# Eight modulation units moved from the front of a two-block transformer kernel into its projection and attention steps

## The reference, cut to what matters

```python
def first_block(x, c, ..., ada_w, ada_b, w_in, ...):
    c_act = jax.nn.silu(c)
    mod = c_act @ ada_w[l] + ada_b[l]
    sh1, sc1, g1, sh2, sc2, g2 = jnp.split(mod, 6, axis=-1)
    h = rmsnorm(x, norm1_g[l]) * (1.0 + sc1[:, None]) + sh1[:, None]
    x = x + g1[:, None] * token_mixer(h, w_in[l], ...)
    h = rmsnorm(x, norm2_g[l]) * (1.0 + sc2[:, None]) + sh2[:, None]
    x = x + g2[:, None] * moe_ffn(h, ...)
    return rmsnorm(x, final_g)
```

## Time and profile before

| | |
|---|---|
| runs | 3006.77, 3005.53, 2999.02 us; median 3005.53 us |
| profiled execution | 2999.47 us, span 2997.7 us |
| busy | PE 2752.5 us (92%), DVE 1880.2 us (63%), ACT 1278.0 us (43%) |
| clock of TensorE granted | 0.956 of full speed over the span |
| read from HBM | 635.59 MB, 214 GB/s over the span |

### The profile page before, as it was taken

How to read it: one execution, slowest core, us unless ns; L and a number is a source line. 1 busy time by engine, 2 the same in 40 slices (tenths; PEclk the granted TensorE clock), 3 DMA queues, 4 the chain that set the end, 5 groups by cost and what they waited for, 6 DMA issues and landing times.

```text
span 2997.7 us, 36656 instructions
## 1 busy us (share of the span) xinstructions
PE 2752.5 (92%) x14444; PEld 2296.5 (77%) x14444; DVE 1880.2 (63%) x2345; ACT 1278.0 (43%) x1540; POOL 24.4 (1%) x46
## 2 busy tenths in 40 slices
PE   3769999897999999999699898999899999999997
PEld 0258898676788787877499396999778888888886
DVE  6986665566666788898766444444555455445444
ACT  2024543342444577777433053534344444443443
POOL 0000000000000000000000000000000000000000
PEclk9789998797999999999899997999999999999999
DMA  8787674340777899999444252544355655555553
GB/s 326 297 319 262 245 272 165 109 173 33 254 258 248 292 324 370 368 369 370 162 168 169 83 190 89 183 177 182 140 196 168 193 187 194 187 195 190 189 197 112
DMA packets 178526, 644.87 MB, mean 215 GB/s; under 512 B 10923, under 2 KB 10988, under 8 KB 134104
## 3 DMA queue, kind: packets, MB, share of 16 engines
q1 hardware_dynamic: 170208, 593.53, 55.7%
q0 software_dynamic: 5344, 30.93, 2.8%
q10 hardware_dynamic: 2840, 18.56, 1.7%
HBM read 635.59 MB, written 7.39 MB: 214 GB/s over the span
## 4 chain that ended last, share of the span: by engine, by line
PE 73%; DVE 12%; DMA 8%; ACT 3%; issue 2%; DVEq 0%; ACTq 0%; SPq 0%
PE ps L1570 72%; DMA raw<-in_stream 7%; DVE w_lo L914 3%; DVE raw L993 2%; ACT w_hi L579 2%; DVE arena L975 0%; DVE arena L973 0%; DVE arena L1073 0%; DVE arena L1089 0%; DVE arena L1475 0%; DVE h_lo L965 0%; PE ps L1704 0%; DVE arena L1473 0%; DVE arena L1474 0%; PE ps L2061 0%
## 5 line engine op out<-in xcount | busy, mean ns | idle before, releaser
L914 DVE TENSOR_TENSOR w_lo<-raw,w_hi 128x1024 fp32r<-128x1024 f32 x968 | 1171.4, 1224 | 803.6 <-ACT w_hi L579 801.0
L579 ACT ACTIVATE w_hi<-raw 128x1024 fp32r<-128x1024 f32 x968 | 1011.8, 1057 | 946.3 <-PE ps L1570 853.2
L1570 PE MATMUL ps<-w_hi,h_hi 128*128 128x512 f32 x1216 | 477.0, 392 | 16.2 <-DVE h_lo L1529 10.0
L1570 PE MATMUL ps<-w_hi,r_hi 128*128 128x512 f32 x1184 | 469.2, 396 | 13.9 <-DVE w_lo L914 5.7
L1570 PE MATMUL ps<-w_lo,h_hi 128*128 128x512 f32 x1216 | 475.0, 391 | 0.0
L1570 PE MATMUL ps<-w_hi,h_lo 128*128 128x512 f32 x1216 | 475.0, 391 | 0.0
L1570 PE MATMUL ps<-w_hi,r_lo 128*128 128x512 f32 x1184 | 462.8, 391 | 0.0
L1570 PE MATMUL ps<-w_lo,r_hi 128*128 128x512 f32 x1184 | 462.8, 391 | 0.0
L1570 PE MATMUL ps<-h_hi,w_hi 128*128 128x256 f32 x1536 | 441.6, 287 | 11.5 <-DVE h_lo L965 3.9
L1570 PE MATMUL ps<-h_lo,w_hi 128*128 128x256 f32 x1536 | 438.1, 285 | 0.0
L1570 PE MATMUL ps<-h_hi,w_lo 128*128 128x256 f32 x1536 | 437.9, 285 | 0.0
(11 more groups left out here) (270 smaller groups left out, 1898.1 us busy)
## 6 DMA issues: line engine op xcount, KB each, us to landing
raw<-in_stream SPq DMA_DIRECT2D x524, 1024.0 KB, 5.5
under_r<-in_stream SPq DMA_DIRECT2D x80, 512.0 KB, 5.2
arena<-in_mod_units ACTq DMA_DIRECT2D x16, 1024.0 KB, 4.8
filters<-arena POOLq DMA_DIRECT2D x4, 1280.0 KB, 5.3
arena<-filters POOLq DMA_DIRECT2D x4, 1280.0 KB, 6.0
x<-in_x POOLq DMA_DIRECT2D x1, 2048.0 KB, 19.7
arena<-bias_rows POOLq DMA_DIRECT2D x2, 1024.0 KB, 6.3
x<-bias_rows POOLq DMA_DIRECT2D x2, 1024.0 KB, 10.5
```

Source lines behind the costliest of these rows:

```text
L579: act.activation(dst, src, ACT.Copy).then_inc(hi_ready, 1)
L914: dve.tensor_tensor(low, src, high, ALU.subtract).then_inc(lo_ready, 1)
L1570: return pe.matmul(o, a, b, start=start, stop=stop)
```

## The change

`FIRST_UNITS` goes from 40 to 32, so that the front does units 0 to 31 alone: one and four units for each `b` in place of one and six. Units 32 to 39 become 16 more asides, and `ASIDE_HALVES` goes from 80 to 96. Sixteen of them stay in attention D, so that the steps 0 to 79 hold 80 in place of 64.

```diff
-FIRST_UNITS = 40
+FIRST_UNITS = 32
 ASIDE_HALVES = 2 * (ADA_UNITS - FIRST_UNITS)
...
         beside = 24 <= k < 32 or 48 <= k < 56 or 72 <= k < 80
-        counts.append(1 if beside or k % 3 < 2 else 0)
+        counts.append((2 if k % 8 in (1, 4, 6) else 1) if beside else 1 if k % 6 else 0)
     counts[GAP_AT] += ASIDE_HALVES - FOURTH_HALVES - sum(counts)
...
                 modulation(done_units, 1)
                 if b < 3:
                     make_taps(b + 1, 2, 4)
-                modulation(done_units + 1, 6)
-                done_units += 7
+                modulation(done_units + 1, 4)
+                done_units += 5
```

## The result

The change makes the kernel slower: 3013.5 us median against 3001.5 us of the kernel before in the same runs (18 of each), a ratio of 1.0042 with a 95% interval of 1.0035 to 1.005. By the ratio that is 12.6 us, by the two medians 12.0. The profiled execution took 3013.62 us (span 3011.8) against 2999.47 us.

What follows compares the result with a forecast made beforehand. VectorE alone was taken to bound the front, TensorE the projections, a loop of three engines the attentions. -18.1 + 3.9 + 1.0 + 1.7 + 1.5 = -10.0 us gave 2995.5 us against the median of 3005.53; range 2988 to 3004.

Steps and rivals of the forecast that it cites:

- Front, -18.1: Front loop: eight units and two additions fewer on VectorE save 18.3 us, less 0.2 us of waiting.
- rival 3: Front: TensorE delivers the sum of absolute values later, so the reciprocal waits about 2 us per b; -4 us, 3001.5, 8%.
- The gap, 0: Gap before attention B: four halves leave, but they ended before VectorE's 8.20 us wait for TensorE, so 0 us.
- Attention B, +3.9: Attention B: three more halves in the loop cost 3.4 us of VectorE, one more pair of additions 0.5 us.
- Attention A, +1.0: Attention A: three more halves make head 7 about 2.8 us late; less 1.8 us of margin, TensorE stops 1.0 us.
- C, +1.7: Attention C: head 7 about 3.2 us late with one more pair of additions; 1.5 us, plus 0.2 for `lo`.
- Three halves are 3.4 us: Attention A: the three added halves priced at 1.14 us of VectorE each.
- The margin of 1.8 us: Attention A: head 7's exponentials end at 306.5 us and TensorE takes them at 308.32, 1.8 us later.
- The projections, +1.5 for all: All three projection stretches: denser asides on two slots stop TensorE for 1.5 us together, near the lower end.
- A sign of being wrong that I had named: Projections: TensorE stops of over 1 us before `w_lo` would show the prediction wrong.
- Rival 2: Projections A and small: single late asides hold up `lo`, 3 to 5 us beyond the sum; -6 us, 2999.5, 20%.
- Rival 4: Projections: two aside slots set the pace; with landings 0.5 us longer TensorE loses 21 us, sum +9.5, 3015; 6%.

Runs made afterwards that it cites:

- e_short_load: The changed kernel with only 64 of 1024 columns of each aside loaded, VectorE's operation in full on the vector alone; 2999.6 us, ratio 0.999.
- g_att: The changed kernel with the sparser old table in the projections, 11 halves in attentions A, C and B, 8 moved to attention D; 3001.2 us, ratio 0.9999.
- s_after_short: The changed kernel with asides ahead of `lo` in the attentions and 64 of 1024 columns of each aside loaded; 2990.4 us, ratio 0.9955.
- v_mend: v_spread with its pause in asides one half step earlier, 58 to 60 instead of 59 to 61; 2994.1 us, ratio 0.9976.
- v_spread: The changed kernel with its 16 added halves spread over C's keys and values, between attentions C and B, and attention D; 2999.0 us, ratio 0.9991.
- v_d28: The changed kernel with the old table up to attention C, 12 halves between C and B, 6 in the gap, 28 in attention D; 2990.3 us, ratio 0.996.
- v_d28_b: v_d28 with the asides ahead of `lo` in attention B alone; 2990.4 us, ratio 0.9961.
- e_front: The kernel before with units 32 to 39 left out of the front, zeros in their place, and no asides added; 2983.8 us, ratio 0.9938.
- e_late16: The changed kernel with the 16 added halves in attention D, two in each step, the old table elsewhere; 2992.9 us, ratio 0.9968.
- f_proj: The changed kernel with the denser table in the projections only, 8 halves each in attentions A, C and B, 8 moved to attention D; 3003.9 us, ratio 1.0006.
- v_36: The kernel before with only four units moved out of the front, their 8 halves in attention D; 2996.0 us, ratio 0.9978.
- s_before: The kernel before with asides ahead of `lo` in its attentions; 3002.5 us, ratio 0.9999.
- s_late16: e_late16 with asides ahead of `lo` in the attentions, in attention D one of the two; 3004.1 us, ratio 1.0006.

## Why the prediction was wrong

- *Front, -18.1:* right. 115.8 became 97.8 us, the reciprocal at b = 0 starts at 88.31 us without a wait behind the additions ahead of it, and rival 3 is out.
- *The gap, 0:* right. From TensorE's first gap matmul to attention B's first scores it took 22.97 us in both kernels.
- *Attention B, +3.9:* 5.0 measured, the term 1.1 us short. Its mechanism, VectorE's operation in the loop, is what e_short_load shows (3.8 us left without the transfers).
- *Attention A, +1.0, and C, +1.7:* the step that failed most, 8.4 us each. "Three halves are 3.4 us" priced an aside there as VectorE's operation alone, and head 7 was to be 2.8 us late. It was 8.9 us late in A. The aside's transfer was priced only in the projections. g_att shows 4.4 and 5.4 us for the density in the attentions, with the transfer gone 3.7 and 2.3 of the 8.4 are left (e_short_load), with the transfer gone and the order turned nothing in A (s_after_short), and the chain has 42% of transfers in A and 21% in C. The second part that I left out is VectorE's lead at the entry: before it came to attention A 3.6 us early, now its first maximum starts 4.6 us later in A and 4.9 later in C. v_mend puts a price on it, 3.0 us in attention C with the old density. The margin of 1.8 us was read for a VectorE that enters 3.6 us early.
- *The projections, +1.5 for all:* 11.7 us measured (2.7 in A, 2.4 in the keys and values of C, 6.6 in the small ones). "Near the lower end, since TensorE's 64.9 of 65 us is the nearest row" was the wrong reading: a TensorE that is never idle shows that the reserve is enough at the density of before, not how much is left of it. The rows that spoke were VectorE's 11.8 us of waits for asides and the round trip of 3.8 us against one aside wanted each 3.5. A sign of being wrong that I had named came: stops of over 1 us before `w_lo` (1.8 in A, 2.5 in the small ones). And VectorE's waits for asides in A were 19.4 us, not 12 to 16.
- *The clock* stood in no term. Each stop of about 3 us at the end of attentions A and C was followed by some 7 us at the lower level. The 2.4 us in the keys and values of C are that. In the small projections (58 us at 0.92) the clock accounts for about 4.5 of the 6.6 us: 2.8 behind attention C's stop and 1.7 behind the stop of 2.5 us.

Rival 2, single late asides, is the 1.8 us in A and the 2.5 in the small projections, a small part of the miss. Rival 4, the slower one, named the right mechanism and came within 1.5 us of the time (3015), and I gave it 6%. That its sum fits so well is luck. It put 21 us into the projections and 6.6 into the attentions. Measured it is 11.7 and 21.8: the slots held VectorE up in the projections, part of what that cost came out in the attentions, and the slots held it up there as well. Whether more than two slots would give all of it back wasn't tried.

The Trainium skill ("DMA: Bandwidth & Descriptors", Specifications) puts the limit of HBM for one core at about 358 GB/s. I had weighed that and left it out of the sum, and wrote that the trace of before stays under it. On the average of the stretches it does. Beside GpSimd's load it doesn't, neither before (first row) nor after (second row):

```profile
414.00:419.00 5.00, 5.00 (x44) 5.00 (x43) 3.78 (x5) 2.77 (x4) 0.00 (x0) 1.00 1.01 419
```

```profile
422.00:427.00 5.00, 4.84 (x41) 4.63 (x39) 0.10 (x1) 2.04 (x3) 0.00 (x0) 1.00 1.02 405
```

So the trace does not agree with that limit for this kernel on its one core, 419 GB/s against 358. Projections A moved 320 GB/s on average and the small ones 307, less than before, so the average load is not what held them up. But at the long landing the DMA engines were busy all the time (1.02), and there full engines are the nearer explanation than a late issue. In projections A they were busy 0.90, and how much of a landing there is queueing no run separates.

## What to carry to other kernels

Work that fills a gap beside other engines has two prices, its operation and its round trip (wait for the slot, transfer, operation). Here the second was paid where the work stood denser than round trip over slots, also in stages that seemed to have room. An engine that is never idle tells nothing of its reserve: look at how far the engine that feeds it runs ahead at each stage's entry, and at what the chain would hold if that lead were gone. Before moving a small transfer, look at what other queues issue at that moment, and at how much the waiting engine has done ahead for the others: with the same late landing, one half step earlier or later was worth 5 us (v_spread and v_mend).

## What the runs showed of the hardware

A small transfer can take as long to land as a large one. In e_short_load 32 KB on SyncE's queue took 10.7 us while GpSimd's 3.2 MB were on the way. The 1024 KB unit issued on the same queue 1.1 us ahead of it took 9.2 us, so the small one landed 2.7 us behind it. Later in the stage such a unit took 4.7 us and the 32 KB after it 2.7. The least in this kernel was 1.6 us. Which part of the 10.7 us is the other queue's load and which the unit ahead, no run separates.

The clock fell at the start of attentions in which TensorE then ran without a stop. v_d28 and v_d28_b have the same instructions in the same order up to attention B. TensorE was busy all through attention C in both, and it took 50.7 us in one and 47.6 in the other:

```profile
338.00:388.66 50.66, 50.66 (x329) 43.82 (x329) 28.56 (x67) 21.55 (x57) 0.00 (x0) 0.93 0.51 186
```

```profile
338.47:386.03 47.56, 47.56 (x328) 41.18 (x329) 28.38 (x67) 21.55 (x57) 0.00 (x0) 1.00 0.51 189
```

The 3.1 us come from some 7 us at the lower level (0.50, 1.2 GHz) from the attention's start on. In e_front, e_short_load, e_late16, f_proj, v_36, v_spread, s_before and s_late16 it was 3.4 us in attention A, and the attention took about 1.5 us longer by it, as here in e_front:

```profile
244.00:250.00 6.00, 5.93 (x29) 5.27 (x30) 1.62 (x4) 3.14 (x6) 0.00 (x0) 0.72 0.53 218
```

TensorE had stood for 1.2 us at the start of attention A and 1.5 us at that of C, in the kernels with the drop and in those without. What decides between the two is open. So an attention's length in the tables is uncertain by 1.5 to 3.1 us. The 8.4 us of the change stand clear of that, since the clock's part in them is small (0.99 over the attention); the differences of 1 to 3 us between single stages do not.
